# Sliding attention: the product of probabilities with values and ones, as one product of 128 stationary columns or as two of 64

## The reference, cut to what matters

```
def swa_sink_mixer(h, k, v, w_q, sinks, w_out):
    ...
    sc = jnp.einsum('bnqgrd,bnkgd->bgrnqk', qb, kk).astype(jnp.float32) * (HEAD_DIM ** -0.5)
    ...
    e = jnp.exp(sc - mx)
    p = e / (e.sum(axis=-1, keepdims=True) + jnp.exp(sink - mx))
    o = jnp.einsum('bgrnqk,bnkgd->bnqgrd', p.astype(vv.dtype), vv)
    return o.reshape(b, s, N_HEADS * HEAD_DIM) @ w_out
```

## Time and profile before

| | us |
|---|---|
| median of 3 runs | 1951.48 (1951.35 to 1952.79) |
| span of the profiled execution, first to last instruction | 1949.0 |
| PE busy | 1929.1 |
| weight loads busy | 1558.9 |
| VectorE busy | 1386.0 |
| ScalarE busy | 974.9 |
| products of L1914, from the first one's start to the last one's start | 1478.7 to 1528.8 |

### The profile page before, as it was taken

The page is one execution under the profiler, slowest core; times in us unless marked ns, Lnnn a source line. Parts: engine busy times, 40 slices in busy tenths (PEclk is TensorE's granted clock), DMA queues, the critical chain, the costliest instruction groups (busy, mean ns, idle before and its releaser), DMA issues.

```text
span 1949.0 us, 26810 instructions
## 1 busy us (share of the span) xinstructions
PE 1929.1 (99%) x9038; PEld 1558.9 (80%) x9038; DVE 1386.0 (71%) x2195; ACT 974.9 (50%) x1422; POOL 26.8 (1%) x47
## 2 busy tenths in 40 slices
PE   9999999999999999999999999999999999999998
PEld 9987888887777788877778888888886688888887
DVE  7986444467999865867746888873388678888534
ACT  5667333456777524577755343333266543333322
POOL 0000000001000000000000000000011000000000
PEclk9999999999999999999999999999999999999999
DMA  5220333326999435400003323333341133233332
GB/s 192 88 65 12 98 97 97 97 98 234 359 356 355 142 98 157 130 20 3 3 3 108 97 97 97 97 97 108 108 119 50 44 97 97 95 94 97 103 107 88
DMA packets 69115, 219.41 MB, mean 113 GB/s; under 512 B 12128, under 2 KB 15360, under 8 KB 68896
## 3 DMA queue, kind: packets, MB, share of 16 engines
q1 hardware_dynamic: 64720, 212.46, 33.5%
q10 hardware_dynamic: 4304, 5.77, 1.2%
HBM read 209.05 MB, written 2.10 MB: 108 GB/s over the span
## 4 chain that ended last, share of the span: by engine, by line
PE 90%; DVE 6%; ACT 2%; issue 1%; ACTq 0%; DMA 0%; SPq 0%; DVEq 0%
PE psum L1074 61%; PE psum L1570 7%; PE psum L1764 4%; PE psum L1544 2%; PE psum L1589 1%; PE psum L1481 1%; PE psum L1553 1%; PE psum L1735 1%; PE psum L1242 1%; PE psum L1690 1%; PE psum L1914 1%; PE psum L1733 1%; PE psum L1624 1%; DVE w_lo L2934 1%; DVE sig L3209 1%
## 5 line engine op out<-in xcount | busy, mean ns | idle before, releaser
L1074 PE MATMUL psum<-x_hi,w_hi 128*128 128x512 f32 (+1 forms) x1344 | 494.1, 378 | 0.0
L1074 PE MATMUL psum<-x_hi,w_lo 128*128 128x512 f32 (+1 forms) x1344 | 490.1, 375 | 0.0
L1074 PE MATMUL psum<-x_lo,w_hi 128*128 128x512 f32 (+1 forms) x1344 | 490.0, 375 | 0.0
L2934 DVE TENSOR_TENSOR w_lo<-raw,w_hi 128x1024 fp32r<-128x1024 f32 x243 | 296.3, 1220 | 187.9 <-ACT w_hi L2036 187.6
L2036 ACT ACTIVATE w_hi<-raw 128x1024 fp32r<-128x1024 f32 x243 | 255.8, 1055 | 190.1 <-DMA raw<-stream 189.4
L1074 PEld LDWEIGHTS psum<-x_hi,w_hi 128*128 128x128 f32 x1344 | 246.5, 188 | 47.4 <-issue 1.9
L1074 PEld LDWEIGHTS psum<-x_lo,w_hi 128*128 128x128 f32 x1344 | 246.5, 188 | 46.0 <-issue 1.4
L1074 PEld LDWEIGHTS psum<-x_hi,w_lo 128*128 128x128 f32 x1344 | 246.4, 188 | 45.8
L1074 PE MATMUL psum<-hid_hi,w_hi 128*128 128x512 f32 (+2 forms) x710 | 261.2, 375 | 0.3 <-DVE hid_lo L4114 0.3
L1074 PE MATMUL psum<-hid_hi,w_lo 128*128 128x512 f32 (+2 forms) x710 | 259.7, 373 | 0.0
L1074 PE MATMUL psum<-hid_lo,w_hi 128*128 128x512 f32 (+2 forms) x710 | 259.6, 373 | 0.0
(11 more groups left out here) (648 smaller groups left out, 2964.6 us busy)
## 6 DMA issues: line engine op xcount, KB each, us to landing
raw<-stream SPq DMA_DIRECT2D x251, 512.0 KB, 3.6
raw<-experts SPq DMA_DIRECT2D x70, 512.0 KB, 5.2
raw_more<-experts SPq DMA_DIRECT2D x68, 512.0 KB, 5.3
staged<-staged ACTq DMA_DIRECT2D x64, 64.0 KB, 3.2
out_fm<-resid SPq DMA_DIRECT2D x7, 256.0 KB, 2.2
resid<-x_fm SPq DMA_DIRECT2D x3, 528.0 KB, 7.3
consts<-consts_in SPq DMA_DIRECT2D x1, 1373.0 KB, 13.5
staged<-staged SPq DMA_DIRECT2D x20, 64.0 KB, 2.8
```

Source lines behind the costliest of these rows:

```text
L1074: last = pe.matmul(o, wt[:, slot, k * P:(k + 1) * P], m[part], start=start and p == 0, stop=stop and p == 2, skip_group_check=True)
L2934: dve.tensor_tensor(w_lo[:, slot, :], raw[:, slot, :], w_hi[:, slot, :].bitcast(F32), ALU.subtract)\
```

## The change

The one product of 128 stationary columns is made as two of 64 columns: the first gives rows 0 to 63 of the bank from the slice's first 64 columns, the second rows 64 to 127 from the other 64. Moving operand, flags and results are the same. The first product carries the waits, the second the increment.

```diff
@@ -1911,8 +1911,11 @@
                 if first and x >= 2:
 
                     pe.wait_ge(wo_kept, x - 1)
-                pe.matmul(window_out_bank(x), VW[:, t - back, g * HD:g * HD + P], PW[q][:, n % 4, :], start=first, stop=back == 0, skip_group_check=True)\
-                  .then_inc(wpv_done, 1)
+                for side in range(2):
+                    column = (g + side) * HD
+                    mm = pe.matmul(window_out_bank(x)[side * HD:(side + 1) * HD, :], VW[:, t - back, column:column + HD], PW[q][:, n % 4, :],
+                                   start=first, stop=back == 0, skip_group_check=True)
+                mm.then_inc(wpv_done, 1)
```

## The result

| | before | after |
|---|---|---|
| median of 8 runs, us | 1951.62 (1951.24 to 1955.75) | 1957.39 (1956.97 to 1962.49) |
| span of the profiled execution, us | 1949.0 | 1955.6 |
| granted clock, mean | 0.999 | 0.999 |
| stretch from the first L1901 matmul to the second L1074 matmul behind the quads, us | 1529.50 - 1476.21 = 53.29 | 1535.87 - 1476.52 = 59.35 |

A forecast was written before the change was run, and what follows sets the result against it. The prediction took PE to bound both quads of sliding attention. It summed +12.0 for overlap of the halves, +9.4 for changing the array's division and -1.5 for waits to +19.9 us, a time of 1971.4, range 1958.5 to 1985.

The forecast's parts named there:

- The bound: In both quads of sliding attention PE is the bound, busy 24.84 of 25.50 us and 26.76 of 27.40.
- If PE starts matmuls in the order of its list, the second half's first matmul can start only when the first half's second one has: Overlap of the halves in each of 28 pairs: 0.43 us more per pair, 12.0 us in all.
- lies in the middle of the bounds: Reason given for the overlap term of 12.0 us, between bounds of 0 and 24.1.
- three lengths: A pair's four matmuls hold PE for three matmul times, 1.29 us, 0.43 more than the whole product.
- Change of the array's division: Going into and out of the divided array around the pairs: 48 new changes at 0.195 us, 9.4 us.
- the upper bound: Most that changing the array's division could cost: 52 changes at the whole gap of 0.22 us, 11.4 us.
- PE's waits: PE's existing waits in the two quads absorb between 1.2 and 1.9 us of new work; 1.5 taken.
- In the first quad PE becomes the later one: Where PE waits for VectorE in the first quad, 0.6 us, PE would now arrive later.
- Rival 2: The halves run side by side entirely, division still paid: +7.9 us, 1959; chance 0.16.
- 1.95 for rival 2: Sign: a step from scores to scores of 1.95 us would mean halves entirely side by side, division paid.
- Rival 4: Not slower: halves entirely side by side and changing the division free, a pair holding PE 0.86 us: 1951.5; chance 0.05.

The follow-up runs named there:

- first experiment: The changed kernel with its two halves written on two source lines, so that the trace names each matmul's half: 1957.76 us.
- second experiments: Products issued twice: first half in the changed kernel, 1986.37 us; both halves in the changed kernel, 1980.74; whole product in the kernel before, 1972.51.
- the kernel with three halves: The changed kernel with the first half's product issued twice, then the second half once: 1986.37 us.
- fifth experiment: The kernel before with its eight products of 36 stationary columns, outside the sliding attention, taken as plain float32 instead of float32r: 1956.37 us.

## Why the prediction was wrong

**The bound** was right. PE's list is what counts: the stretch grew by 6.06 us, and outside of it little moved.

**"If PE starts matmuls in the order of its list, the second half's first matmul can start only when the first half's second one has"**: this is the step that failed. The term was 28 x 0.43 = 12.0 us, and it measures 0. The first and second experiments show the second half's first matmul starting about 0.01 us behind the first half's first one, past one matmul of the list (past three in the kernel with three halves). The strict order was an assumption: no row of before had two parts in use at once. The reason given for it, that it "lies in the middle of the bounds", was no reason: either the list's order holds between the halves or it doesn't, and no row spoke for three lengths.

**Change of the array's division**: the term was 48 x 0.195 = 9.4 us. Taking L1924 and not L1513 as the nearest row was right, and the fifth experiment says why. The size was a little high: a whole way in and out costs 0.35 for a division by columns (1.90 - 1.56, 3.46 - 3.10 and 3.39 - 3.04) instead of 0.39, and at the four steps that already had L1924 the pair adds 0.15 us (2.56 against 2.41) instead of the 0.195 of one way. The count missed one more neighbour of that sort: in the first quad L1885 (32 stationary columns, float32) stands behind a pair, and that step grows by 0.26 us only (1.99 to 2.25). That makes 21 x 0.35 + 0.26 + 4 x 0.15 = 8.2 us. In the upper bound the gap of 0.22 is 0.20 by its own numbers (1513.04 to 1513.24), so 10.4 instead of 11.4; nothing else hung on it.

**PE's waits** absorb 8.2 - 6.06 = 2.1 us, where 1.5 was taken and 1.9 was the bound. No row of them is left between the matmuls of the two quads in the profile of after; with the whole product twice 2.6 us were absorbed. Counting the rows of waits, plus 0.16 each, reads too little; the steps say more. From one L1902 to the next, five steps of before are longer than others with the same work: 2.72, 2.47 and 2.29 us against 2.01 (steps with maxima), and 2.11 and 2.10 against 1.56. That is 2.5 us in which PE was held up. In after four of the five have the length of their like (2.36, 2.37, 1.91, 1.90) and the first is still 0.37 over (2.74 against 2.37), held up by VectorE's queries for the second quad: 2.5 - 0.4 = 2.1. "In the first quad PE becomes the later one" was thus right but for one step.

**The sum by these sizes** is 0 + 8.2 - 2.1 = +6.1 in the quads, and with the 0.5 us outside of them the 6.6 of the spans. Rival 2 had this mechanism and gave 1959; it came within 1.6 us. Of the section of the Trainium skill named there, the rule on side-by-side columns leads to rival 2 and held; its rule on the order of matmuls (first experiment) would have led to the forecast and did not hold. So the section alone could not choose between them, and a row with two parts in use at once was what was missing. The result fell a microsecond below the range because the range left rival 2 only one microsecond of room, while the division cost 1.2 less and the waits absorbed 0.6 more than rival 2 was priced with. The signs by which the text meant to be judged did their work: "1.95 for rival 2" for a plain step, with a gap ahead of the next scores' load, and 1.90 with the gap was measured.

**Rival 4** (not slower) fell by the price of the division. Even with it gone nothing would have been gained: the pair holds PE for 0.86 us in either form.

## What to carry to other kernels

Splitting a full-width product over two parts of PE's array gains nothing where PE is the bound: the halves do run side by side, but two halves take as long as the whole, and going into the divided array and out again costs about 0.35 us each time it stands between whole-array work. So look for the reverse: a product of few rows among whole-array ones (a spread, a selection) is cheaper over all 128 rows with zeros in the unused ones: 0.3 to 0.4 us at nearly each of the 27 places here and 9.7 us in the whole kernel. Where narrow products are needed, put them behind one another, so that the way in and out is paid once.

## What the runs showed of the hardware that was not expected

- Matmuls in different column positions overtake each other. A matmul of the second half starts 0.42 to 0.47 us before one of the first half that stands ahead of it in the list (experiment 1), and in the kernel with the first half twice three stood ahead of it that had not started.
- Loads into the two column positions stand less than 0.01 us apart although both use all 128 rows, and all four loads of a pair are issued within 0.06 us (1509.61 to 1509.67).
- A change between whole and divided array is paid for columns (0.32 to 0.36 us for in and out) nearly as for rows (0.33 to 0.44 at most places). No load runs ahead across it. "TensorEngine Tiling (Array Packing)" of the Trainium skill, section "Key Properties", says that changing the tiling mode drains the engine; the loads without a lead agree.
- With few stationary columns, float32 and float32r behave differently: the same 36-column products have gaps of 0.35 and 0.84 us in the loads at their ends in float32, and in float32r the first load runs ahead by 0.22 us as usual and no time is lost on either side.
